# Input projection computed tile by tile inside the norm loop, in a decoder layer on eight cores

## The reference

```python
h = rmsnorm(x, pre_mix_g[l])
proj = h @ w_in[l]                       # 2048 -> 4368 columns
q_a, k_a, v_a, q_b, k_b, v_b, f_b = jnp.split(proj, cuts, axis=-1)
o_a = swa_sink_attention(q_a, k_a, v_a, sinks[l])        # window 128, 16 heads, 2 kv heads
log_f = jax.nn.log_sigmoid(f_b + b_forget[l])
o_b = forgetting_attention(q_b, k_b, v_b, log_f)         # full causal, 16 heads
...                                      # group norms, output projection, residual
u = causal_dwconv(h @ w_up[l], conv_w[l], conv_b[l])     # second half: GeGLU MLP, d_ff 5632
```

## Time and profile before

| what | value |
|---|---|
| runs shown | 5327.52 and 5572.95 us, median 5450.23 |
| the profiled execution | 5317.33 us, span 5315.4 us (core 7, the slowest) |
| spans of the eight cores | 5259.2 to 5315.4 us |
| TensorE, share of the span busy | 78% |
| ScalarE, VectorE, POOL | 37%, 35%, 10% |
| chain that ended last | PE 48%, DMA 33%, issue 7%, DVE 6%, ACT 3% |
| both projection passes, from the first load of x to the last matmul of line 489 | 24.1 to 1012.8 us |

### The profile page before, as it was taken

The page is one execution under the profiler, slowest core; times in us unless marked ns, Lnnn a source line. Parts: engine busy times, 40 slices in busy tenths (PEclk is TensorE's granted clock), DMA queues, the critical chain, the costliest instruction groups (busy, mean ns, idle before and its releaser), DMA issues.

```text
span 5315.4 us, 67575 instructions; the slowest of 8 cores (5259.2 to 5315.4 us)
## 1 busy us (share of the span) xinstructions
PE 4122.5 (78%) x22672; PEld 2003.0 (38%) x22672; DVE 1835.6 (35%) x1928; ACT 1990.7 (37%) x4119; POOL 544.6 (10%) x461
## 2 busy tenths in 40 slices
PE   2796999654876998779488795975888869758887
PEld 2474545531433444334233342432333323323333
DVE  3014111221654442246344403543442135434422
ACT  3014000132852442079134404962442069524420
POOL 0000000000002111200111120002111200021112
PEclk9896999855987999889789997987999989879998
DMA  7746445156346998843689894346998843469988
GB/s 171 102 94 169 74 79 89 48 122 127 91 100 106 126 121 120 137 111 90 117 110 125 111 153 115 101 96 106 120 127 116 138 132 108 75 102 123 124 124 138
DMA packets 719458, 602.97 MB, mean 113 GB/s; under 512 B 28395, under 2 KB 701567, under 8 KB 706287
## 3 DMA queue, kind: packets, MB, share of 16 engines
q0 software_dynamic: 573536, 365.36, 51.7%
q1 hardware_dynamic: 145587, 233.30, 14.6%
HBM read 908.13 MB, written 55.78 MB: 181 GB/s over the span
## 4 chain that ended last, share of the span: by engine, by line
PE 48%; DMA 33%; issue 7%; DVE 6%; ACT 3%; POOL 1%; SPq 1%; DVEq 0%; POOLq 0%; ACTq 0%
DMA t<-w_up 25%; PE p L965 12%; PE p L421 9%; PE p L727 7%; PE p L715 5%; PE p L442 5%; PE p L812 4%; DMA t<-w_out 2%; PE p L917 2%; ACT t L335 1%; DVE t L981 1%; DMA t<-alhi 1%; DVE t L601 1%; ACT t L719 1%; DMA t<-w_in 1%
## 5 line engine op out<-in xcount | busy, mean ns | idle before, releaser
L917 PE MATMUL p<-t 128*128 128x512 bf16 x5632 | 1309.6, 394 | 160.5 <-DMA t<-w_up 137.3
L719 ACT ACTIVATE t<-p 128x512 bf16<-128x512 f32 (+3 forms) x1920 | 892.8, 532 | 168.3 <-PE p L715 112.2
L917 PEld LDWEIGHTS p<-t 128*128 128x128 bf16 x5632 | 557.1, 101 | 870.9 <-issue 286.0
L715 PE MATMUL p<-t 71*128 71x512 bf16 (+1 forms) x1648 | 595.0, 375 | 221.1 <-DMA t<-qfT 142.0
L727 PE MATMUL p<-t 128*128 128x512 bf16 (+3 forms) x1920 | 679.6, 359 | 57.2 <-DMA t<-vf 24.5
L965 PE MATMUL p<-t 128*128 128x512 bf16 x2816 | 616.8, 383 | 59.7 <-DMA t<-w_down 59.7
L928 DVE SCALAR_TENSOR_TENSOR t<-t 128x512 f32<-128x512 f32 x352 | 264.5, 751 | 815.4 <-ACT t L925 438.3
L920 ACT ACTIVATE t<-p 128x512 f32<-128x512 f32 x352 | 210.6, 598 | 863.8 <-PE p L917 752.5
L421 PE MATMUL p<-t 128*128 128x512 bf16 (+1 forms) x2432 | 496.9, 369 | 38.7 <-DMA t<-w_in 36.7
L965 PEld LDWEIGHTS p<-t 128*128 128x128 bf16 x2816 | 277.2, 99 | 399.3 <-issue 73.0
L727 PEld LDWEIGHTS p<-t 128*128 128x128 bf16 x1920 | 192.0, 100 | 480.3 <-issue 426.6
(11 more groups left out here) (95 smaller groups left out, 3408.8 us busy)
## 6 DMA issues: line engine op xcount, KB each, us to landing
t<-w_up POOLq DMA_DIRECT2D x176, 1024.0 KB, 11.8
t<-w_down POOLq DMA_DIRECT2D x176, 512.0 KB, 7.3
t<-xx SPq DMA_DIRECT2D x49, 1024.0 KB, 8.9
t<-w_out POOLq DMA_DIRECT2D x20, 2048.0 KB, 21.5
t<-w_in POOLq DMA_DIRECT2D x34, 1024.0 KB, 12.5
vf<-t SPq DMA_DIRECT2D x128, 128.0 KB
out<-t SPq DMA_DIRECT2D x16, 1024.0 KB
t<-vf SPq DMA_DIRECT2D x8, 2048.0 KB
```

Source lines behind the costliest of these rows:

```text
L715: P.op("pe", lambda e: e.matmul(S[:, 0:W], lhsT=kt[0:71, j * 128:(j + 1) * 128], rhs=qt[0:71, 0:W], start=True, stop=True), r=[Rkt, Rqt], ...
L719: P.op("act", lambda e: e.activation(out=PT[:, c0:W], in_=S[:, c0:W], func=AF.Exp), r=[RS], w=[RPT])
L917: P.op("pe", lambda e, ps=ps, c=c, Wu=Wu, part=part, wo=wo: e.matmul(ps[:, :], lhsT=Wu[:, c, part * 256 + wo:part * 256 + wo + 128], rhs=h ...
```

## The change

`hT` gets one `Res` for each tile of 512 tokens instead of one in all. The weights of the first three chunks of each pass are requested ahead of the norm loop, and those three chunks are computed inside it: after the transposes of blocks 3, 7, 11 and 15, the tile of 512 tokens that has just become complete is multiplied with all three. The other 15 chunks follow after the loop, each over all four tiles as before. In the context pass the chunks are taken in another order: 4 and 9 to 17 first, the eight query chunks last; the early ones there are 4, 9 and 10, in the second pass 0, 1 and 2. No buffer is added and no arithmetic is changed.

```diff
-                RhT = Res()
+                RhT = [Res() for _ in range(TP // 512)]
...
-                    pend = None
-                    for tb in range(ntok // 128):
-                        ...
-                        if pend is not None:
-                            transpose_block(*pend)
-                        pend = (hb, Rhb, hT, RhT, tb * 128, tpring, tb)
-                    transpose_block(*pend)
...
                     def fm(Wt, RW, col_lo, tiles, scale, dest_fn):
                         for (t0, tw) in tiles:
                             ps, Rps = mmring.next()
+                            Rh = RhT[t0 // 512]
...
-                                    start=(c == 0), stop=(c == 15)), r=[RW, RhT], w=[Rps])
+                                    start=(c == 0), stop=(c == 15)), r=[RW, Rh], w=[Rps])
...
-                    for ch in range(18):
-                        ...
-                        Wt, RW, dW = wring.next()
-                        ncol = 256 if ch < 17 else 16
-                        P.dma("pool", Wt[:, :, 0:ncol], w_in_v[:, :, ch * 256: ch * 256 + ncol], dW, w=[RW])
+                    def do_chunk(ch, Wt, RW, tsel):
+                        ft = full_tiles if tsel is None else [full_tiles[tsel]]
+                        tbs = range(ntok // 128) if tsel is None else range(tsel * 4, tsel * 4 + 4)
...
+                    order = ([4, 9, 10, 11, 12, 13, 14, 15, 16, 17, 0, 1, 2, 3, 5, 6, 7, 8] if is_ctx
+                             else list(range(18)))
+                    NE = 3
+                    early = [(ch,) + load_chunk(ch) for ch in order[:NE]]
+
+                    def after_block(b):
+                        if (b + 1) % 4 == 0:
+                            for (ch, Wt, RW) in early:
+                                do_chunk(ch, Wt, RW, b // 4)
+
+                    pend = None
+                    for tb in range(ntok // 128):
+                        xs, Rxs, dxs = xring.next()
+                        P.dma("sp", xs[:], xx[tok0 + tb * 128: tok0 + (tb + 1) * 128, :], dxs, w=[Rxs])
+                        rstd, Rs = norm_stats(xs[:], Rxs, junk, Rjunk, small)
...
+                        if pend is not None:
+                            transpose_block(*pend)
+                            after_block(tb - 1)
+                        pend = (hb, Rhb, hT, RhT[tb // 4], tb * 128, tpring, tb)
+                    transpose_block(*pend)
+                    after_block(ntok // 128 - 1)
+
+                    for ch in order[NE:]:
+                        Wt, RW = load_chunk(ch)
+                        do_chunk(ch, Wt, RW, None)
```

More of the change, by code:

```diff
@@ L396, in build_program @@
                 for (tok0, ntok, is_ctx) in passes:
-                    pend = None
-                    for tb in range(ntok // 128):
[L399 to L405, removed]
-                        if pend is not None:
-                            transpose_block(*pend)
-                        pend = (hb, Rhb, hT, RhT, tb * 128, tpring, tb)
-                    transpose_block(*pend)
+                    ntile = ntok // 512
                     full_tiles = [(t0, 512) for t0 in range(0, ntok, 512)]
@@ L435, in fm, with tm @@
                                 P.dma("sp", dest_fn(hh, t0, tw), stg[hh * 64:(hh + 1) * 64, 0:tw], dstg, r=[Rstg])
-                    def tm(Wt, RW, col_lo, nheads, dst, dcol0):
+                    def tm(Wt, RW, col_lo, nheads, dst, dcol0, tbs):
                         ncols = nheads * 64
-                        for tb in range(ntok // 128):
+                        for tb in tbs:
                             ps, Rps = mmring.next()
+                            Rh = RhT[tb // 4]
                             for c in range(16):
@@ L444, in tm @@
                                     rhs=Wt[:, c, col_lo:col_lo + ncols], start=(c == 0), stop=(c == 15)),
-                                    r=[RW, RhT], w=[Rps])
+                                    r=[RW, Rh], w=[Rps])
                             vst, Rvst, dvst = vstring.next()
@@ L467, in build_program @@
                             h0 = (ch if ch < 4 else ch - 5) * 4
-                            tiles = halo_tiles if is_ctx else full_tiles
+                            if is_ctx:
+                                tiles = halo_tiles if (tsel is None or tsel == ntile - 1) else []
+                            else:
+                                tiles = ft
                             for sub in range(2):
@@ L473, in build_program @@
                         elif ch == 4:
-                            fm(Wt, RW, 0, full_tiles, 1.0,
+                            fm(Wt, RW, 0, ft, 1.0,
                                lambda hh, t0, tw: kaT[hh, 0:64, tok0 + t0: tok0 + t0 + tw])
-                            tm(Wt, RW, 128, 2, va, 0)
+                            tm(Wt, RW, 128, 2, va, 0, tbs)
                         elif 9 <= ch <= 12:
@@ L479, in build_program @@
                             for sub in range(2):
-                                fm(Wt, RW, sub * 128, full_tiles, 1.0,
+                                fm(Wt, RW, sub * 128, ft, 1.0,
                                    lambda hh, t0, tw, h0=h0, sub=sub:
@@ L483, in build_program @@
                         elif 13 <= ch <= 16:
-                            tm(Wt, RW, 0, 4, vf, (ch - 13) * 4 * 128)
+                            tm(Wt, RW, 0, 4, vf, (ch - 13) * 4 * 128, tbs)
                         else:
-                            for (t0, tw) in full_tiles:
+                            for (t0, tw) in ft:
                                 ps, Rps = mmring.next()
+                                Rh = RhT[t0 // 512]
                                 for c in range(16):
@@ L498, in build_program, with load_chunk @@
                                     r=[Ret], w=[RspT])
+                    def load_chunk(ch):
+                        Wt, RW, dW = wring.next()
+                        ncol = 256 if ch < 17 else 16
+                        P.dma("pool", Wt[:, :, 0:ncol], w_in_v[:, :, ch * 256: ch * 256 + ncol], dW, w=[RW])
+                        return Wt, RW
+                    order = ([4, 9, 10, 11, 12, 13, 14, 15, 16, 17, 0, 1, 2, 3, 5, 6, 7, 8] if is_ctx
[11 more added lines that the diff above has]
+                        rstd, Rs = norm_stats(xs[:], Rxs, junk, Rjunk, small)
+                        hb, Rhb = hbring.next()
+                        P.op("dve", lambda e, hb=hb, xs=xs, rstd=rstd: e.scalar_tensor_tensor(
+                            out=hb[:], in0=xs[:], scalar=rstd[:, 0:1], in1=gpre[:], op0=ALU.mult, op1=ALU.mult),
+                            r=[Rxs, Rs, Rg], w=[Rhb])
+                        if pend is not None:
[7 more added lines that the diff above has]
+                        do_chunk(ch, Wt, RW, None)
             with P.scope():
```

2 lines of the change are left out of this document (removed).

## The result

The changed kernel took a median of 5422.21 us in 11 runs, the kernel before 5439.38 us in 10, the two shown at the start among them. The change makes the kernel slower by 1.7%. The profiled execution took 5408.9 us.

What follows compares the result with a forecast made beforehand. In the norm stage no engine is full; a chain of norm, transposes and copies sets the pace. Restarts and clock 85.1, query chunks 1.6, weights 0.6, pass change 10.4 sum to 97.7 on 5317.3: 5415 us, range 5385 to 5540.

Steps and rivals of the forecast that it cites:

- (a): After each early group, stores go out, then x lands before the next norm: 11.3 us context pass, 8.5 second.
- (b): Restarting the norm chain: 22.3 us from norm to the tile's last copy against 19.6 running, 2.7 added each.
- (c): TensorE's matmuls start at the lower clock after a pause: 1.9 us a start, five more starts, 9.5 us.
- (d): Query chunks at the context pass's end can't cover their weight loads: 59.6 us against 58 before, 1.6 added.
- (e): Fourth chunk's weights arrive 0 to 0.6 us after the last early group, twice; 0.6 taken in all.
- (f): Between passes, query stores stand ahead of x: 11.8 us to the first norm, less 1.4 before, 10.4 added.
- the rival called no change: Loads of x run ahead of the groups, so the 59.4 us of waiting vanish: 5356 us; chance 0.07.
- the rivals of less loss or of a gain: Cheap restarts with x already loaded, 5356 us, chance 0.07; groups hidden under the norm chain, 5213 us, chance 0.03.
- The dearer restart: Four loads of x after a group are served side by side, 15.6 us: 5460 us, over 2% slower; chance 0.37.
- groups are hidden by themselves: Norm chain runs on under three 21 us groups a pass, saving 126 less 22: 5213 us; chance 0.03.

Runs made afterwards that it cites:

- the first comparison: The changed kernel measured against the kernel before, the first time: ratio 1.0175, 95% interval 1.0125 to 1.0224.
- the repetition: The same changed kernel measured once more against the kernel before: ratio 1.0169, interval 1.0149 to 1.0188.
- the kernel with x ahead: Changed kernel with loads of x issued four blocks ahead, before the group's stores: passes' end 1057.1 us, repeated 1059.1; ratio 1.0155 to the kernel before.

## Why the prediction came out as it did

**The time and the mechanism.** 5415 us were forecast on an execution of 5317.3, a ratio of 1.0184; ratios of 1.0169 and 1.0175 came. The median of 5422 lies near 5415 by luck, for the kernel before had a median of 5439 beside it, not 5317. Term by term, from the slowest core's trace:

| term | predicted, us | in the trace, us |
|---|---|---|
| (a) last matmul to norm, context pass | 11.3 each | 9.6, 9.4, 8.9 |
| (a) second pass | 8.5 each | 8.5, 7.2, 7.9 |
| (b) norm to last copy of the tile | 22.3 each | 22.1, 22.1, 18.6 in each pass |
| (c) start at the lower clock | 1.9 each | 1.5 to 2.3 |
| (d) query chunks at the end | 59.6 | 58.0 |
| (e) wait for the fourth chunk's weights | 0.6 | 0 |
| (f) last query matmul to the first norm | 11.8 | 12.6 |
| sum, passes' end | 97.7 | 89.7 (median of cores 88.9) |

The mechanism was right, and the term that was mis-sized is (a): its six waits are 51.5 us in the trace where 59.4 were forecast, which is the 8 us too many. I took the context pass's landing of x, 9.5 us, from a stretch in which loads followed one another without a pause. After a group no other load of x is under way, and x came in 6.8 to 7.4 us (85.88 to 93.28 is the first), in the second pass in 5.2 to 6.2. The nearer row for such a load was the 6.7 of the earlier trace rows, in both passes. The other terms were off by less and nearly cancel: (b), (d) and (e) were some 4 us too high, (f) and the clock's starts some 2 too low, and 2 are assigned to nothing. In (b), only three norms stand behind the third restart, not four: 18.6 us. Added up, these three stretches are 62.8 us a pass; from the first tile's last copy to the pass's last it took 55.8 (context pass) and 55.3 before, so starting the chain cost 7.0 and 7.5 a pass, not 8.1.

That the restarts are the loss was shown by leaving them out pass by pass (41.1 to 44.7 and 39.2 of the 88.9 us), and that waiting for x is half of it by asking for x earlier, which gave back 42.7 us. The 66 us from pieces in place of groups are more than the rest: besides the restarts they count work that is now hidden.

**Where it was wrong: the last step, from the sum to the numbers.** It failed in two places. *The base.* The sum of 97.7 us was put on the profiled execution, 5317.3, while the upper end of the range was reckoned for a median like the one shown, 5450; "I don't move the sum for that", it says. Set beside that median, 5415 reads as a kernel 0.6% faster, and the arithmetic says 1.8% slower. The runs showed how little such medians tell: they went from 5439.38 down to 5422.21 us while the ratio was 1.0175. The forecast should have been given as a ratio. *What a measurement can tell.* The chances were divided at 2%, with the words that 2% is about what a measurement of this kernel can tell from no change, and so a forecast of 1.8% slower was filed as "within 2%", 0.60, together with the rival called no change, beside 0.37 for slower. But the interval was 0.5% wide on either side in the first comparison and 0.2% in the repetition. A loss of 1.7% stands clear of both. The arithmetic was for "slower", the rivals of less loss or of a gain had 0.10 together, and the forecast should have said so: I took the scatter of the two runs shown for what a comparison of many can resolve.

**Rivals.** The dearer restart (5460) did not come: the first of four loads came in 7.4 us at most, where side by side would have been 15.6, and none of the later ones was waited for. That loads run ahead of the groups (5356) is what the kernel with x ahead did once the order allowed it, and its passes ended 46 us behind those before, 38 by that rival's sum. That groups are hidden by themselves (5213) needed another order; written out, with pieces, lag and late evacuation, it gave 0.9884.

**The rules.** For a load from rest the trace has 5.2 to 7.4 us for 1 MB. The Trainium skill's fit in "DMA: Bandwidth & Descriptors", section on the anatomy of one DMA, would be an estimate of 4.4, below all of them; part of the gap may be that eight cores load at once, which no run here took away. The fit is for loads issued from GpSimd, and these are SP's. At the start of the second pass, with the weight loads of its first three chunks requested before it, x took 10.6 us (484.25 to 494.89) where I had 10.5. By the same page of the Trainium skill, section on queues, rings and completion order, each DMA engine takes turns between queues packet by packet. If such turns were equal shares, 13.4 would be the estimate; the trace doesn't agree with equal shares, and turns by packet need not be equal, so this doesn't speak against the rule itself. That the loads slow each other the traces do show (24.3 us for chunk 7's weights beside x, 13.4 for a chunk's weights without it).

## What to carry to other kernels

Splitting a dependency lets work overlap only if every engine, and the queue that issues the loads, has something else to do at that place in its order: read what stands behind the moved block on each engine before counting any gain. Work meant to fill gaps should come in pieces no longer than the gap, one step behind the data that frees them, with loads issued ahead of the stores of a piece, though not so many that those stores are held in turn, and evacuations behind the next step of the chain they would block. And when a forecast lies near a limit, give it as a ratio and ask what the comparison can resolve, not what single runs scatter.

## What the runs showed that I had not expected

- Requesting 4 MB of x earlier is not free: stores behind it held ScalarE for 19.49 us and TensorE for 11.88, about as much as the 13.3 us of waiting for weights that it took away.
- Transposes between dense matmuls cost half: 16 of them took 1.06 us (granted clock 0.95 over that stretch) and 1.9 to 2.1 in the norm stage alone (0.53 in the second pass), so filling the gap also shortened them.
- The chip matters nearly as much as the change. The kernel before had medians of 5323.55 and 5319.84 us on two chips and 5253.44 and 5269.14 on two others. The difference lies behind the passes, 4275 to 4307 us on the median core in the traces of the first two and 4228 to 4236 on the others, while the passes' end repeats to some 5 us or less. So a total is compared only with one taken on the same chip.
